# Layer four of a streaming encoder step: pooled projection, gate projection and group matmul alternated tile by tile

## The chip, the cores and the metric
One Trainium2 chip, all 8 cores, one program. Each core computes its own half of one prompt (2048 positions and their halo) and one sample request; the cores do not exchange data. The time is that of the slowest core, in microseconds of device time.

## The reference, cut to what matters
The trunk has four layers, each `x = x + gate * out`, with a different mixer. The layer in question is the fourth, multi-scale pooling:

```
h = rms_norm(x, g_norm[3]) * (1 + scale) + shift                  # 1024 channels
pv, z = split(h @ w_in_d, 2)                                       # 2048 channels each
ext = concat(history of 15 rows, pv)
dlt = trailing mean of ext over 2 / 4 / 8 / 16 rows (by channel group of 512) - pv
y = (dlt @ w_pool_d[g], for each of the four groups) * scale_pool_d
out = (y * silu(z)) @ w_out_d                                      # back to 1024
```
The last 15 rows of `ext` are outputs as well. Layers one to three and the final RMSNorm are unchanged.

## The kernel before
Channels lie on partitions, positions along the free axis. A core has 2128 positions (`NX`), in five tiles `t` with bounds `TB` (432, 384, 384, 512 and 416 columns; layer four leaves out the first 32 or 48 columns, so that its first tile has 400 or 384). The 2048 branch channels are 16 chunks `c` of 128; a pooling group `g` has four chunks, its window is `2 << g`.

The engines' instruction streams are written by one Python program in one order. `Sched` keeps for each named buffer who wrote it and who read it and adds semaphore waits; each engine then runs its own stream in that order. A buffer's key stands for the whole buffer, and keys whose memory overlaps exclude each other. Matmul results go through six PSUM banks in rotation (`next_bank`); banks 6 and 7 hold sums of squares.

Weights of 128 x 1024 come by GpSimd's queue into a ring of 20 slots in the order of `plan`; `done` gives a slot back, and the ring frees only from its oldest slot on.

Layer four before, for each group: a stage of pooled projections (four chunks by five tiles, eight matmuls each, `proj` and `mm8`, L458), a stage of gate projections (the same with Silu on the way out, L1047), a stage of group matmuls (four matmuls each, over the four pooled chunks `DL`, with the gate product L1059 on VectorE). In the pooled stage a tile goes through

- L1010 VectorE: copy the last 15 columns of the tile before into the head of this tile's buffer `tf` (L1007, a memset, for the first tile)
- L1012 ScalarE: evict the bank into `tf` behind the head (twice in the last tile, which has a second history for the sample)
- L1015, L1019, L1020, L1021 VectorE: mask, second history, rows to be kept (first or last tile only)
- L1027 VectorE: `g + 1` adds that double the window each time
- L1032 VectorE: scale and subtract into `DL[i]`; L1037 and L1039 correct the first 16 positions

The copy and the eviction write the same key `tf`, so the eviction waits for the copy. There are two `tf` buffers, and one set of four `DL` buffers that lies over the x buffers `XT` of the output projection. `out_proj` (L569 matmuls, L577 residual add, L507 square, L508 sum of squares) loads x tiles `xbuf` into these by SyncE's queue; after its last matmul of layer three it normalises the last tile into `HT` (L515, L516, L524, L526), which layer four's last tile reads.

Of the kernel before, what the change touches and what calls it, by code (L numbers as in the profile page):

```python
# [7 lines left out]
ALU = mybir.AluOpType  # L8
# [6 lines left out]
NX = 2128  # L15
HALO = 48
SMP = 2096
# [189 lines left out]
def build_program():  # L207
# [175 lines left out]
    for g in range(4):  # L383
        for j in (0, 1):
            for i in range(4):
                add(("in", 3, 16 * j + 4 * g + i), w_in_d[3][16 * j + 4 * g + i])
        for hf in range(2):
            add(("pool", g, hf), w_pool_d[2 * g + hf])
# [597 lines left out]
    def layer_d():  # L986
        TF = [tmp("tf%d" % i, i * 528, 528) for i in range(2)]
        SA = tmp("sa", 1056, 528)
        SB = tmp("sb", 1584, 528)
        T3 = tmp("t3", 2112, 16)  # L990
        DL = [xsb("dl%d" % i, 8192 - 1064 * (i + 1), NX, True) for i in range(4)]
        n = 0
        for g in range(4):
            win = 2 << g
            for i in range(4):
                c = 4 * g + i
                od = outD[c % 2]
                for t in range(NT):
                    x0, x1 = max(TB[t], 32), TB[t + 1]
                    w = x1 - x0  # L1000
                    tf, tf_old = TF[n % 2], TF[(n + 1) % 2]
                    n += 1
                    tail = (t == NT - 1)
                    b = proj(3, c, t, 32)
                    parts = [(0, w, 15)] if not tail else [(0, SMP - x0, 15), (SMP - x0, w, 30)]
                    if t == 0:
                        s.op("dve", lambda h, tf=tf: h.memset(tf.v[:, 0:15], 0.0), writes=[tf.key])  # L1007
                    else:
                        pw = x0 - max(TB[t - 1], 32)
                        s.op("dve", lambda h, tf=tf, tf_old=tf_old, pw=pw: h.tensor_copy(out=tf.v[:, 0:15], in_=tf_old.v[:, pw:pw + 15]), reads=[tf_old.key], writes=[tf.key])  # L1010
                    for (a, e, sh) in parts:
                        s.op("act", lambda h, b=b, tf=tf, a=a, e=e, sh=sh: h.activation(out=tf.v[:, a + sh:e + sh], in_=bank(b)[:, a:e], func=AF.Copy), reads=[], writes=bk(b) + [tf.key])  # L1012
                    wx = w + 15
                    if t == 0:
                        s.op("dve", lambda h, tf=tf: h.tensor_scalar_mul(out=tf.v[:, 15:31], in0=tf.v[:, 15:31], scalar1=maskc[:, 0:1]), reads=["par", tf.key], writes=[tf.key])  # L1015
                    if tail:
                        wx = w + 30
                        pe_ = SMP - x0 + 15
                        s.op("dve", lambda h, tf=tf, c=c, pe_=pe_: h.tensor_copy(out=tf.v[:, pe_:pe_ + 15], in_=stD[:, c, :]), reads=["par"], writes=[tf.key])  # L1019
                        s.op("dve", lambda h, tf=tf, pe_=pe_, od=od: h.tensor_copy(out=od[:, 0:15], in_=tf.v[:, pe_ - 15:pe_]), reads=[tf.key], writes=["outD%d" % (c % 2)])  # L1020
                        s.op("dve", lambda h, tf=tf, wx=wx, od=od: h.tensor_copy(out=od[:, 15:30], in_=tf.v[:, wx - 15:wx]), reads=[tf.key], writes=["outD%d" % (c % 2)])  # L1021
                        s.dma("sp", "o_d%d" % (c % 2), opd[c], od, reads=["outD%d" % (c % 2)], writes=["O.pd.%d" % c])
                    src, lo, sh = tf, 0, 1
                    for k in range(g + 1):
                        dst = SA if k % 2 == 0 else SB
                        lo2 = lo + sh
                        s.op("dve", lambda h, src=src, dst=dst, lo2=lo2, sh=sh, wx=wx: h.tensor_tensor(out=dst.v[:, lo2:wx], in0=src.v[:, lo2:wx], in1=src.v[:, lo2 - sh:wx - sh], op=ALU.add),  # L1027
                             reads=[src.key], writes=[dst.key])
                        src, lo, sh = dst, lo2, sh * 2
                    outs = [(max(a, 48 - x0), e, p) for (a, e, p) in parts]  # L1030
                    for (a, e, p) in outs:
                        s.op("dve", lambda h, src=src, tf=tf, a=a, e=e, p=p, i=i, x0=x0, win=win: h.scalar_tensor_tensor(  # L1032
                            out=DL[i].v[:, x0 + a:x0 + e], in0=src.v[:, a + p:e + p], scalar=1.0 / win, in1=tf.v[:, a + p:e + p], op0=ALU.mult, op1=ALU.subtract),
                            reads=[src.key, tf.key], writes=[DL[i].key])
                    if t == 0:
                        o = 15 + 16
# [3 lines left out]
                             reads=[T3.key, tf.key], writes=[DL[i].key])  # L1040
                done(("in", 3, c))
            for i in range(4):
                c = 4 * g + i
                for t in range(NT):
                    x0, x1 = max(TB[t], HALO), TB[t + 1]
                    b = proj(3, 16 + c, t, HALO)
# [130 lines left out]
```

How the kernel before makes its waits and increments, by code:

```python
        def emit(h):  # L128
            for sm, v in wl:
                h.wait_ge(sm, v)
            ins = fn(h)
            ins.then_inc(mysem, 1)
# [18 lines left out]
        def emit(h):  # L151
            for sm, v in wl:
                h.wait_ge(sm, v)
            h.dma_start(out=out, in_=in_).then_inc(dsm, 16)
# [9 lines left out]
        def emit(h):  # L164
            for sm, v in wl:
                h.wait_ge(sm, v)
```

## Time and profile before

| | us |
|---|---|
| median of 3 runs (lowest to highest) | 2855.18 (2853.37 to 3117.13) |
| the profiled execution | 2853.27 |
| its span on the slowest core (core 2) | 2851.7 |
| spans of the eight cores | 2838.4 to 2851.7 |
| mean granted TensorE clock, cores | 0.913 to 0.920 |
| layer four in the span | 2236.8 to 2674.5 |
| last output projection | from 2674.5 |

A clock of 1.00 is TensorE at 2.4 GHz, 0.50 at 1.2 GHz. In the rows, PE is TensorE's matmuls, PEld its weight loads, DVE VectorE, ACT ScalarE, POOL GpSimd, SP SyncE; `big` is SBUF, `ps` PSUM.

### The profile page before, as it was taken

What the parts mean: (1) busy time and instruction counts of PE and PEld (TensorE: products, weight loads), DVE (VectorE), ACT (ScalarE), POOL (GpSimd) and SP (SyncE); (2) the same over time, 40 slices, a digit from 0 to 9 for tenths busy, and PEclk for the clock granted to TensorE, in tenths of its full rate; (3) what the DMA queues carried; (4) which work ended last, traced back from release to release, by engine and by line L of the source; (5) the groups of instructions that cost most, each with busy time, mean ns of one, the idle gap of its engine ahead of it and who ended that gap; (6) DMA issues with size and microseconds to landing.
All of it is one profiled execution on the core that took longest, in us unless ns stands there. A gap on an engine that the chain in (4) does not pass through costs nothing.

```text
span 2851.7 us, 38831 instructions; the slowest of 8 cores (2838.4 to 2851.7 us)
## 1 busy us (share of the span) xinstructions
PE 2253.8 (79%) x12651; PEld 1200.2 (42%) x12651; DVE 1498.8 (53%) x2600; ACT 778.4 (27%) x1381; POOL 198.4 (7%) x373
## 2 busy tenths in 40 slices
PE   1396899977899999878688888867578687685976
PEld 0142555543455555443345454533243343341543
DVE  1466562233666666533566666567633444757343
ACT  2621233333311111132322222256522322121211
POOL 1001201100010101000000000000000100000000
PEclk9998899988999999988799998988788899897998
DMA  9300727534343433424543334234433421111132
GB/s 185 98 1 4 119 34 130 85 100 103 55 63 50 60 52 52 78 80 125 103 78 78 78 78 78 60 83 116 112 110 115 83 31 27 23 27 15 49 110 86
DMA packets 142851, 215.10 MB, mean 75 GB/s; under 512 B 14560, under 2 KB 83168, under 8 KB 141920
## 3 DMA queue, kind: packets, MB, share of 16 engines
q0 software_dynamic: 50544, 96.00, 22.8%
q1 hardware_dynamic: 92112, 116.63, 13.4%
q8 instruction: 106, 1.74, 0.2%
q14 instruction: 89, 0.73, 0.1%
HBM read 255.18 MB, written 53.40 MB: 108 GB/s over the span
## 4 chain that ended last, share of the span: by engine, by line
PE 58%; DVE 19%; ACT 10%; issue 6%; DMA 5%; POOL 1%; DVEq 1%; ACTq 0%; SPq 0%; POOLq 0%
PE ps L458 37%; PE ps L569 15%; DVE big L1027 4%; ACT big L526 3%; DVE big L516 2%; ACT big L953 2%; DVE big L681 2%; DVE big L1032 2%; ACT big L1012 2%; PE ps L508 2%; PE ps L879 1%; DVE big L915 1%; DMA big<-w_ada 1%; DVE big L524 1%; DMA big<-xbuf 1%
## 5 line engine op out<-in xcount | busy, mean ns | idle before, releaser
L458 PE MATMUL ps<-big 128*128 128x384 bf16 (+4 forms) x7360 | 1417.7, 352 | 206.7 <-ACT big L1012 104.4
L458 PEld LDWEIGHTS ps<-big 128*128 128x128 bf16 x7360 | 723.9, 100 | 841.0 <-issue 305.2
L569 PE MATMUL ps<-big 128*128 128x384 bf16 (+4 forms) x2560 | 522.7, 363 | 20.7 <-DVE big L966 20.7
L569 PEld LDWEIGHTS ps<-big 128*128 128x128 bf16 x2560 | 263.6, 103 | 255.8 <-issue 70.7
L577 DVE SCALAR_TENSOR_TENSOR big<-ps,big 128x384 f32<-128x384 f32 (+3 forms) x192 | 110.2, 582 | 406.6 <-PE ps L569 376.4
L507 ACT ACTIVATE big<-big 128x384 bf16<-128x384 f32 (+4 forms) x200 | 107.9, 554 | 510.1 <-DVE big L577 463.0
L508 PE MATMUL ps<-big 128*128 128x384 bf16 (+4 forms) x200 | 75.3, 397 | 211.3 <-ACT big L507 211.3
L915 DVE TENSOR_TENSOR big<-big,ps 128x384 bf16<-128x384 f32 (+1 forms) x96 | 160.1, 1668 | 106.0 <-ACT big L911 103.0
L526 ACT ACTIVATE big<-big 128x384 bf16<-128x384 f32 (+3 forms) x192 | 131.3, 684 | 94.8 <-DVE big L524 78.6
L1027 DVE TENSOR_TENSOR big<-big 128x398 f32<-128x398 f32 (+11 forms) x200 | 121.9, 610 | 57.6 <-ACT big L1012 42.4
L674 PE MATMUL ps<-big 128*128 128x512 bf16 (+1 forms) x576 | 129.2, 387 | 10.0 <-ACT big L677 5.4
L508 PEld LDWEIGHTS ps<-big 128*128 128x128 bf16 x200 | 20.2, 102 | 246.2 <-issue 235.4
L516 DVE RECIPROCAL big<-big 128x384 f32<-128x384 f32 (+4 forms) x25 | 70.3, 2812 | 101.5 <-ACT big L515 101.5
L818 ACT ACTIVATE big<-ps 128x384 bf16<-128x384 f32 (+3 forms) x80 | 42.0, 526 | 289.2 <-PE ps L458 289.1
L1012 ACT ACTIVATE big<-ps 128x384 f32<-128x384 f32 (+1 forms) x96 | 44.3, 462 | 270.4 <-DVE big L1010 177.5
L822 DVE SCALAR_TENSOR_TENSOR big<-big 128x384 f32<-128x384 f32 (+3 forms) x160 | 106.2, 664 | 17.0 <-DVE big L820 0.5
L879 PE MATMUL ps<-big 128*128 128x270 bf16 x640 | 108.9, 322 | 0.0
L807 DVE TENSOR_TENSOR big<-big,ps 128x384 f32<-128x384 f32 (+1 forms) x96 | 50.3, 524 | 99.0 <-PE ps L458 89.0
L886 ACT ACTIVATE big<-ps,big 128x270 bf16<-128x270 f32 x128 | 62.3, 486 | 140.4 <-DVE big L889 70.0
L911 ACT ACTIVATE big<-ps 128x384 f32<-128x384 f32 (+3 forms) x80 | 42.1, 527 | 210.5 <-PE ps L458 169.4
L893 PE MATMUL ps<-big 128*128 128x270 bf16 x128 | 40.3, 316 | 74.0 <-ACT big L886 73.5
L855 DVE TENSOR_TENSOR big<-big 128x1280 bf16<-128x1280 bf16 x64 | 94.7, 1486 | 2.0 <-PE ps L894 0.5
(105 smaller groups left out, 1678.9 us busy)
## 6 DMA issues: line engine op xcount, KB each, us to landing
big<-w_ada POOLq DMA_DIRECT2D x96, 256.0 KB, 6.6
big<-w_in_b POOLq DMA_DIRECT2D x64, 256.0 KB, 6.6
big<-w_in_c POOLq DMA_DIRECT2D x48, 256.0 KB, 5.4
big<-xbuf SPq DMA_DIRECT2D x7, 1536.0 KB, 8.9
xbuf<-big SPq DMA_DIRECT2D x48, 192.0 KB, 2.0
gbuf<-big SPq DMA_DIRECT2D x16, 548.0 KB, 6.3
big<-gbuf SPq DMA_DIRECT2D x16, 548.0 KB, 4.9
ybuf<-big SPq DMA_DIRECT2D x16, 540.0 KB, 2.7
```

Source lines behind the costliest of these rows:

```text
L458: ins = h.matmul(out, lhsT=lhs(k), rhs=rhs(k), start=(k == 0), stop=(k == n - 1))
L507: s.op("act", lambda h: h.activation(out=SQ[k].v[:, 0:w], in_=XT[q][d].v[:, 0:w], func=AF.Square), reads=[XT[q][d].key], writes=[SQ[k].key])
L508: return lambda: s.op("pe", lambda h: h.matmul(bank(b)[:, 0:w], lhsT=onesb, rhs=SQ[k].v[:, 0:w], start=(d == 0), stop=(d == 7)), reads=["o ...
L516: s.op("dve", lambda h: h.reciprocal(out=R.v[:, 0:w], in_=R.v[:, 0:w]), reads=[R.key], writes=[R.key])
L526: s.op("act", lambda h, X=X, d=d, a=a, b=b, sq=sq: h.activation(out=HT[:, d, 80 + a:80 + b], in_=X.v[:, a - x0:b - x0], func=AF.Identity, ...
L569: ins = h.matmul(bank(b)[:, 0:w], lhsT=w8[e // 8][:, e % 8, :], rhs=YS[:, e, x0:x0 + w], start=(e == 0), stop=(e == 15))
L577: s.op("dve", lambda h, b=b, X=X, a=a, e=e, sq=sq, d=d, x0=x0: h.scalar_tensor_tensor(out=X.v[:, a - x0:e - x0], in0=bank(b)[:, a - x0:e - ...
L674: ins = h.matmul(bank(p + j)[0:n, :], lhsT=HT[:, kc, c0:c0 + n], rhs=w[:, kc, :], start=(kc == 0), stop=(kc == 7))
L822: s.op("dve", lambda h, P=P, A=A, c=c, wx=wx, j=j: h.scalar_tensor_tensor(out=A.v[:, 0:wx], in0=P.v[:, j:j + wx], scalar=wcb[:, c, j:j + 1 ...
L879: ins = h.matmul(bank(b)[:, 0:YPH], lhsT=W.v[:, o:o + 128], rhs=GP.v[:, g * CPH + 4 - sh:g * CPH + 4 - sh + YPH], start=(sh == 0), stop=(s ...
L915: s.op("dve", lambda h, b=ba, sg=sg, a=a - x0, e=e - x0, m0=m0, M=M, G3=G3: h.tensor_tensor(out=G3[:, :, m0:m0 + M].rearrange("q p m -> q ...
L1027: s.op("dve", lambda h, src=src, dst=dst, lo2=lo2, sh=sh, wx=wx: h.tensor_tensor(out=dst.v[:, lo2:wx], in0=src.v[:, lo2:wx], in1=src.v[:, ...
```

## The change
Groups run in the order 8, 16, 4, 2 (`GORD = (2, 3, 1, 0)`). For each chunk and tile the program now issues a pooled projection with its VectorE work (`pv`), a gate projection (`zgate`), and, from the second group on, a group matmul with gate product of the group before (`pooled`). After the last group its group matmuls follow alone, tile by tile. Two sets `DLS` of four pooled chunks take turns; the first chunk of each set lies in scratch, the others over the x buffers. There are three `tf` buffers instead of two. The eviction is issued ahead of the history copy, and the head of `tf` has a key of its own (`"h" + tf.key`), so that the eviction no longer waits for the copy. The weight plan follows the new order.

```diff
+    GORD = (2, 3, 1, 0)
+    for g in GORD:
+        for i in range(4):
+            for j in (0, 1):
                 add(("in", 3, 16 * j + 4 * g + i), w_in_d[3][16 * j + 4 * g + i])
...
-        TF = [tmp("tf%d" % i, i * 528, 528) for i in range(2)]
+        TF = [tmp("tf%d" % i, i * 528, 528) for i in range(3)]
...
-        DL = [xsb("dl%d" % i, 8192 - 1064 * (i + 1), NX, True) for i in range(4)]
+        DLS = [[tmp("dl0.0", 2656, NX, True)] + [xsb("dl0.%d" % (i + 1), 1064 * i, NX, True) for i in range(3)],
+               [tmp("dl1.0", 3720, NX, True)] + [xsb("dl1.%d" % (i + 1), 8192 - 1064 * (i + 1), NX, True) for i in range(3)]]
...
+            b = proj(3, c, t, 32)
+            parts = [(0, w, 15)] if not tail else [(0, SMP - x0, 15), (SMP - x0, w, 30)]
+            for (a, e, sh) in parts:
+                s.op("act", lambda h, b=b, tf=tf, a=a, e=e, sh=sh: h.activation(out=tf.v[:, a + sh:e + sh], in_=bank(b)[:, a:e], func=AF.Copy), reads=[], writes=bk(b) + [tf.key])
+            if t == 0:
+                s.op("dve", lambda h, tf=tf: h.memset(tf.v[:, 0:15], 0.0), writes=["h" + tf.key])
+            else:
+                pw = x0 - max(TB[t - 1], 32)
+                s.op("dve", lambda h, tf=tf, tf_old=tf_old, pw=pw: h.tensor_copy(out=tf.v[:, 0:15], in_=tf_old.v[:, pw:pw + 15]), reads=[tf_old.key, "h" + tf_old.key], writes=["h" + tf.key])
...
+        for gi, g in enumerate(GORD):
+            for i in range(4):
+                for t in range(NT):
+                    pv(g, i, t, DLS[gi % 2])
+                    zgate(4 * g + i, t)
+                    if gi:
+                        pooled(GORD[gi - 1], i, t, DLS[(gi - 1) % 2])
+                done(("in", 3, 4 * g + i))
+                done(("in", 3, 16 + 4 * g + i))
+            if gi:
+                for hf in range(2):
+                    done(("pool", GORD[gi - 1], hf))
+        g = GORD[-1]
+        for t in range(NT):
             for fi in range(4):
+                pooled(g, fi, t, DLS[1])
+        for hf in range(2):
+            done(("pool", g, hf))
```
Where the diff has no lines, the arithmetic of a tile (mask, adds, subtraction, gate product) is the same as before.

## Rows read from the trace of the kernel before

**Rows 1.** Windows, core 2: engines' busy us, granted clock, DMA share, GB/s

```profile
2300.00:2338.00 38.00, 37.66 (x215) 20.87 (x216) 14.66 (x28) 11.35 (x22) 2.65 (x5) 1.00 0.20 29
...
2550.00:2637.60 87.60, 48.02 (x188) 19.68 (x187) 62.58 (x138) 10.71 (x24) 2.65 (x5) 0.77 0.15 21
...
2238.00:2683.50 445.50, 325.00 (x1630) 161.38 (x1628) 251.87 (x562) 95.52 (x197) 19.51 (x37) 0.90 0.19 32
```

**Rows 2.** Waits, 2238 to 2684 us: us in total, times, longest

```profile
ACT big L1012 <- DVE big L1010: 177.5, 62, 4.3
...
PE ps L458 <- ACT big L1012: 104.4, 59, 3.7
...
DVE big L1027 <- ACT big L1012: 42.4, 48, 7.3
...
DVE big L1019 <- ACT big L1012: 14.6, 15, 1.0
DVE big L1015 <- ACT big L1012: 13.3, 16, 1.3
```

**Rows 3.** Timeline of one tile, window 16: start, duration, instruction

```profile
2577.09 0.17 DVE L1010 COPY big<-big 128x15 f32<-128x15 f32 x1
2577.35 0.49 ACT L1012 ACTIVATE big<-ps 128x384 f32<-128x384 f32 x1 [4.30 <-DVE big L1010]
2577.94 2.58 DVE L1027 TENSOR_TENSOR big<-big 128x398 f32<-128x398 f32 x4 [0.69 <-ACT big L1012]
...
2580.63 0.56 DVE L1032 SCALAR_TENSOR_TENSOR big<-big 128x384 bf16<-128x384 f32 x1
2581.11 0.17 DVE L1010 COPY big<-big 128x15 f32<-128x15 f32 x1
```

**Rows 4.** Windows from one 512-column eviction L1012 to the next, VectorE alone

```profile
2346.15:2362.33 16.18, 10.53 (x27) 0.79 0.14 21
...
2446.57:2466.26 19.69, 13.56 (x32) 0.83 0.10 15
2562.31:2585.38 23.07, 16.56 (x37) 0.88 0.09 12
...
2259.07:2271.56 12.49, 7.47 (x22) 1.00 0.31 43
```

**Rows 5.** Timeline, VectorE, group matmuls' stage of window 4

```profile
2423.00 3.27 DVE L1059 SCALAR_TENSOR_TENSOR big<-ps,big 128x512 bf16<-128x512 f32 x5 [0.24 <-PE ps L458]
```

**Rows 6.** Timeline, ScalarE, gate projections: one tile of two neighbouring chunks

```profile
2407.41 0.49 ACT L1047 ACTIVATE big<-ps 128x384 bf16<-128x384 f32 x1 [0.78 <-PE ps L458]
...
2414.44 0.49 ACT L1047 ACTIVATE big<-ps 128x384 bf16<-128x384 f32 x1 [0.78 <-PE ps L458]
```

**Rows 7.** Timeline, start of layer four

```profile
2255.34 9.84 PE L458 MATMUL ps<-big 128*128 128x416 bf16 x45 [12.49 <-ACT big L526]
2255.57 0.57 DVE L1027 TENSOR_TENSOR big<-big 128x398 f32<-128x398 f32 x1 [7.33 <-ACT big L1012]
```

**Rows 8.** Timeline, start of the last output projection

```profile
2674.46 5.36 PE L569 MATMUL ps<-big 128*128 128x384 bf16 x32
...
2681.69 1.14 DVE L577 SCALAR_TENSOR_TENSOR big<-ps,big 128x384 f32<-128x384 f32 x2 [6.31 <-DMA big<-xbuf]
...
2688.80 2.84 PE L569 MATMUL ps<-big 128*128 128x384 bf16 x16
```

**Rows 9.** Timeline, TensorE, pooled stages of windows 2 and 16

```profile
2280.61 1.46 PE L458 MATMUL ps<-big 128*128 128x384 bf16 x8 [1.27 <-ACT big L1012]
...
2596.64 2.72 PE L458 MATMUL ps<-big 128*128 128x384 bf16 x8 [2.69 <-ACT big L1012]
```

**Rows 10.** Line L818, the Silu of layer two: its table loads

```profile
L818 ACT ACT_TABLE_LOAD  x1: 1283/1283/1283, 737.0 to 737.0; - x1
```

**Rows 11.** Window over layer two, columns as in rows 1

```profile
740.00:1180.00 440.00, 440.00 (x2615) 241.59 (x2614) 293.24 (x640) 79.93 (x152) 44.81 (x84) 1.00 0.36 51
```

**Rows 12.** The page's DMA issues: KB each, us to landing

```profile
big<-w_in_b POOLq DMA_DIRECT2D x64, 256.0 KB, 6.6
```

More of the change, by code:

```diff
@@ L382, in build_program @@
     add_out(2)
-    for g in range(4):
-        for j in (0, 1):
-            for i in range(4):
+    GORD = (2, 3, 1, 0)
+    for g in GORD:
+        for i in range(4):
+            for j in (0, 1):
                 add(("in", 3, 16 * j + 4 * g + i), w_in_d[3][16 * j + 4 * g + i])
@@ L986, in layer_d @@
     def layer_d():
-        TF = [tmp("tf%d" % i, i * 528, 528) for i in range(2)]
-        SA = tmp("sa", 1056, 528)
-        SB = tmp("sb", 1584, 528)
-        T3 = tmp("t3", 2112, 16)
-        DL = [xsb("dl%d" % i, 8192 - 1064 * (i + 1), NX, True) for i in range(4)]
-        n = 0
-        for g in range(4):
-            win = 2 << g
[L995 to L1036, printed above, removed]
-                        s.op("dve", lambda h, src=src, g=g, o=o: h.tensor_tensor(out=T3.v, in0=src.v[:, o:o + 16], in1=invc[:, g * 16:(g + 1) * 16], op=ALU.mult),
-                             reads=[src.key, "par"], writes=[T3.key])
-                        s.op("dve", lambda h, tf=tf, i=i, o=o: h.tensor_tensor(out=DL[i].v[:, 48:64], in0=T3.v, in1=tf.v[:, o:o + 16], op=ALU.subtract),
[L1040 to L1046, printed above, removed]
-                    s.op("act", lambda h, b=b, c=c, x0=x0, x1=x1: h.activation(out=YS[:, c, x0:x1], in_=bank(b)[:, 0:x1 - x0], func=AF.Silu), reads=[], writes=bk(b) + ["ys.%d.%d" % (c, t)])
-                done(("in", 3, 16 + c))
@@ L1049, in layer_d, with zgate, pooled @@
+        def zgate(c, t):
+            x0, x1 = max(TB[t], HALO), TB[t + 1]
+            b = proj(3, 16 + c, t, HALO)
+            s.op("act", lambda h: h.activation(out=YS[:, c, x0:x1], in_=bank(b)[:, 0:x1 - x0], func=AF.Silu), reads=[], writes=bk(b) + ["ys.%d.%d" % (c, t)])
+        def pooled(g, fi, t, DL):
             wp = [use(("pool", g, hf)) for hf in range(2)]
             wpv = [v3(v, 2) for v, _ in wp]
-            for fi in range(4):
-                c = 4 * g + fi
-                for t in range(NT):
-                    x0, x1 = max(TB[t], HALO), TB[t + 1]
-                    w = x1 - x0
-                    b = next_bank()
-                    item(mm8(bank(b)[:, 0:w], lambda k, fi=fi, wpv=wpv: wpv[k // 2][:, k % 2, fi * 128:(fi + 1) * 128], lambda k, x0=x0, x1=x1: DL[k].v[:, x0:x1], 4),
-                         [k for _, ks in wp for k in ks] + [DL[k].key for k in range(4)], bk(b))
-                    s.op("dve", lambda h, b=b, c=c, x0=x0, x1=x1, w=w: h.scalar_tensor_tensor(out=YS[:, c, x0:x1], in0=bank(b)[:, 0:w], scalar=pv_("spool")[:, c:c + 1], in1=YS[:, c, x0:x1],
-                                                                                             op0=ALU.mult, op1=ALU.mult), reads=["par", "ys.%d.%d" % (c, t)], writes=bk(b) + ["ys.%d.%d" % (c, t)])
@@ L1061, in layer_d @@
-            for hf in range(2):
-                done(("pool", g, hf))
+            c = 4 * g + fi
+            x0, x1 = max(TB[t], HALO), TB[t + 1]
+            w = x1 - x0
+            b = next_bank()
+            item(mm8(bank(b)[:, 0:w], lambda k: wpv[k // 2][:, k % 2, fi * 128:(fi + 1) * 128], lambda k: DL[k].v[:, x0:x1], 4),
+                 [k for _, ks in wp for k in ks] + [DL[k].key for k in range(4)], bk(b))
+            s.op("dve", lambda h: h.scalar_tensor_tensor(out=YS[:, c, x0:x1], in0=bank(b)[:, 0:w], scalar=pv_("spool")[:, c:c + 1], in1=YS[:, c, x0:x1],
+                                                         op0=ALU.mult, op1=ALU.mult), reads=["par", "ys.%d.%d" % (c, t)], writes=bk(b) + ["ys.%d.%d" % (c, t)])
```

40 lines of the change are left out of this document (added).

## The prediction

> **What bounds the kernel now.** I first found layer four in the trace. On core 2, the profiled one, it runs from 2236.8 to 2674.5 us of a span of 2851.7 us, and only it and the start of the last output projection are touched by the change. TensorE is busy 325 us of the 445.5 us around it, VectorE 252 us; neither is full [rows 1]. Split by stage, the gate projections and group matmuls run TensorE without a hole (37.66 busy of 38.00 us, clock 1.00), while the pooled projections of the last group leave it 48 us busy in 87.6, at a mean clock of 0.77 [rows 1]. So TensorE idles in one kind of stage and VectorE in the other, and neither idle time is used.
>
> The waits say what sets the pace of the pooled stages. ScalarE's eviction L1012 waited 177.5 us for the history copy L1010, and TensorE 104.4 us for that eviction; VectorE in turn waited for the eviction at L1027, L1019 and L1015 [rows 2]. The timeline of one tile shows the ring: history copy at 2577.09, eviction, four adds from 2577.94, the subtraction at 2580.63, the next copy at 2581.11 [rows 3]. A tile costs 4.02 us there, TensorE's eight matmuls take 1.46 of it at full clock [rows 9]. It is a chain of VectorE work with a round trip over ScalarE in it. A whole chunk (five tiles, from one 512-column eviction to the next) takes 12.49, 16.18, 19.69 and 23.07 us for windows 2, 4, 8 and 16, with VectorE busy 7.47, 10.53, 13.56 and 16.56 us [rows 4].
>
> **The change, part by part.** Number of matmuls, adds, evictions and bytes is the same; work is only reordered, so I price each new stage by the engine that fills it.
>
> *The round trip goes.* The eviction no longer stands behind the copy, and a third buffer lets it run two tiles ahead. VectorE waited for L1012 42.4 + 14.6 + 13.3 us; 7.3 of the first is the start of the layer. The other 63.0 us are 3.94 per chunk [rows 2]. Not all of it returns: the adds now follow the copy on VectorE itself, and between two dependent operations there lie 0.11 us (four adds end at 2577.94 + 2.58 = 2580.52, the next starts at 2580.63) [rows 3]. Five such gaps are 0.55, so a chunk gets 3.4 us shorter: 9.1, 12.8, 16.3 and 19.7 us of VectorE.
>
> *The gate products join in.* L1059 runs five in 3.27 us when it has a backlog [rows 5], 3.3 per chunk. Bounds: between VectorE's own operations they may overlap their neighbours (the subtraction of 0.56 us is followed by the copy after 0.48 [rows 3]), 2.9; or each takes a gap of 0.11 more, 3.8. I take 3.3, the row itself. VectorE per chunk with the gates: window 16 23.0, window 4 16.1, window 2 12.4; window 8, whose chunks come first, 16.3 without them.
>
> *TensorE per chunk.* Evictions of the same tile of two chunks of the gate projection lie 7.03 us apart (2407.41 to 2414.44) with TensorE full [rows 6]. The pooled projection has the same eight matmuls and 16 more columns, 7.1; the group matmul has four of eight, 3.5. Together 17.6, in the first group 14.1.
>
> *Which engine sets each stage.* First group (window 8): VectorE, 16.3 over 14.1. Second (16, with gates of 8): VectorE, 23.0 over 17.6. Third (4): TensorE, 17.6 over 16.1. Fourth (2): TensorE, 17.6 over 12.4. The rest, four chunks of group matmuls: TensorE, 14.1 over 13.2. This needs TensorE to run ahead. Six banks, three per tile, are two tiles of lead; what holds a bank longest is the gate product, which waits for nothing but its own matmul. Of each engine's queue: a late group matmul would hold up VectorE's next adds behind the gate product, but TensorE has it done a tile earlier; ScalarE has two evictions of about 0.5 us in a tile of 3.5 to 4.6 and is not near full.
>
> *Start.* ScalarE normalises the last tile's input after the layer has begun, and TensorE stood 12.49 us for it, until 2255.34 [rows 7]. The new first tile has three adds instead of one ahead of that work (1.35 us later), and a gate eviction and the next pooled eviction behind it, so VectorE resumes at about 2257.6 instead of 2255.6. The time TensorE could gain by gate projections meanwhile is worth nothing, since VectorE sets this group. From there: four chunks less the one tile done, 65.2 - 3.4 = 61.8, to 2319.4; second group 4 x 23.0 = 92.0, to 2411.4. TensorE enters the third group two projections ahead (2.7 us, all it can do before the group matmul needs the last chunk's final tile), but that matmul and the small difference of 17.6 and 16.1 make tiles catch on each other: I book 1.5 us back. 4 x 17.6 = 70.4, to 2480; fourth 70.4, to 2551; 2 us until the last tile's adds are through; 14.1, to 2567. Before: 2674.5. Gain 107.5 us.
>
> *End.* The first of the second chunk set no longer lies over the first x buffer, so x of tile 0 is loaded during the last group matmuls. Before, that load ended the wait at 2681.69, 6.31 us, and TensorE reached its fourth output item at 2688.80, 14.3 us after the first; that item's 16 matmuls took 2.84 [rows 8], so three with their two sum matmuls are 8.8. Gain 5.5. The load of tile 1 still waits for the last group matmul; it is wanted 22 us later, which hides its 7 us. If tile 0's load were not early, the 5.5 us are lost. SyncE's queue holds only the small outputs of kept rows ahead of it.
>
> *Clock.* In the stage of window 2, holes of 1.27 us between tiles [rows 9] went with a granted clock of 1.00 [rows 4]; after a hole of 2.69 us the eight matmuls took 2.72 instead of 1.46 us, half the clock [rows 9]. The new holes are (23.0 - 17.6) / 5 = 1.1 us on average in the second group, smaller elsewhere, but not even, since t3 and t4 differ. A tile at half clock costs TensorE 3.5 us, where it has 1.1 spare. Nothing to 10 us; I take 3, near the rows with small holes. In the third and fourth group there are no holes.
>
> *Free by cover.* The weights: the ring of 20 holds two pool slots, eight, two and eight, so while one group runs, the next one's is loaded; a slot's transfer took 6.6 us [rows 12] on a stage of 65. Evictions alternate Copy and Silu; layer two does the same and shows one table load of 1.283 us in its 455 us [rows 10], and there was one here before too, so nothing is added.
>
> Sum: 107.5 + 5.5 - 3 = 110 us. The profiled execution took 2853.3 us (1.6 beyond the span), the median is 2855.2. 2853.3 - 110 = 2743.3; with half of the 1.9 us between the two, 2744 us.
>
> **A rule of the Trainium skill against this.** In layer two TensorE was full for 440 us on this core, all cores running the same program, at a granted clock of 1.00 [rows 11]; and the 7.03 us per chunk of layer four [rows 6] are its 16640 columns at 2.4 GHz (6.93 us) and little more. The Trainium skill, page TensorE: Matmul & The Clock Gate, Part 1, "What's actually happening", says that once three cores of a die run dense matmuls the die goes to 13/16 of the clock. By that rule layer two would have shown 0.81; the trace disagrees, so the rule has a small chance here, as rival (a).
>
> **Rivals.**
>
> (a) TensorE's rate stays low when the holes close, as all neighbours become dense too. From the layer's own mean, 0.90, to its worst stage, 0.77 [rows 1], chunks of 17.6 become 19.6 to 22.9 us. Third and fourth group and the rest grow by 155 x (1/0.90 - 1) = 17 to 155 x (1/0.77 - 1) = 46 us, the first group by none to 4 x 2.0 = 8: 17 to 54, the middle 36: 2780 us. Against it stands layer two [rows 11]. 0.05. The rule of the Trainium skill, page TensorE: Matmul & The Clock Gate, is of this kind; an estimate from its 13/16 is 40 us, 2784.
>
> (b) The engines catch on each other: banks or the three buffers give less lead than counted, each tile loses 0.4 us (for scale: one step from VectorE's copy to ScalarE's eviction is 2577.09 to 2577.35, 0.26 us [rows 3], and a tile would pay it once or twice). 80 x 0.4 = 32 us: 2776 us. For it: tiles are uneven (384 to 512 columns, more small copies on the last). 0.12.
>
> (c) Weights late: as the group's two pool slots stay held through the next group, ten transfers go out at once at each boundary. If each of four boundaries waited for one landing, 4 x 6.6 [rows 12] = 26 us: 2770 us. 0.03.
>
> (d) The clock falls for good in the VectorE-bound groups: TensorE's chunk is 28.2 and 35.2 us, 4 x (28.2 - 16.3) + 4 x (35.2 - 23.0) = 96 us more: 2840 us, no change that can be told. Against it: at half clock TensorE would be full, and the full stretch from 2300 is at 1.00 [rows 1]. 0.04.
>
> (e) Slower: lock step. VectorE's gate product of a tile waits for its group matmul, that waits in TensorE's order behind two projections, and if the next pooled projection can only start when the gate product frees the bank, each tile is the sum: 3.5 TensorE + 0.5 ScalarE + 2.9 VectorE (mean of the four chunks, over 5) + 0.7 gate = 7.6 us. 80 tiles are 608 us instead of 438: some 3025 us. It decides as soon as the lead falls below one tile, and passes the old time from 5.4 us per tile on. Six banks speak against it. 0.03.
>
> That the change does not do what it says would be (e) or (b) in part.
>
> **Chances and range.** Forecast 0.73, (a) 0.05, (b) 0.12, (c) 0.03, (d) 0.04, (e) 0.03. The forecast's own bounds: gates -2 to +4, clock +3 to -7, hand-over between groups 4, the start 2, all of them rough, 2728 to 2762. To hold (b), (a) and (c) in most of their forms, and a DVE chain cheaper than I price it, the range is 2722 to 2786. Two per cent is what a measurement can tell from no change, 2798 us here: forecast, (a), (b), (c) lie below it, 0.92 with some spill; (d) and spill 0.05; (e) 0.03.
>
> **What would show it.** Right: VectorE over 95% occupied (busy plus its small gaps) in the first two groups, with a 512-column eviction to the next in about 16.3 and 23 us; TensorE full at 1.00 in groups three and four, 17.6 us per chunk; no wait of L1012 for the history copy; no wait of L577 for x. Wrong: VectorE waiting for L1012 or the group matmul in every tile (b, e), a clock below 0.9 in the first two groups (d), chunks of over 20 us with TensorE full (a), TensorE waiting for a weight transfer (c). The number is most exposed in VectorE's 154 us of groups one and two: 5% there are 8 us.

## The result, and the profile after

The changed kernel takes 2733.9 us (median of 4 runs, 2733.5 to 2736.8), against 2855.2 shown before; the ratio is 0.958, with a 95% interval of 0.9557 to 0.9603. The forecast was 2744, its range 2722 to 2786. Of the four runs of the kernel before in that comparison two were at 3112 and 3117 us with a lower clock on one die; they are left out of the ratio.

The page of the slowest core (7), its first lines: span, then each engine's busy time.

```profile
span 2731.4 us, 38776 instructions; the slowest of 8 cores (2721.2 to 2731.4 us)
PE 2212.5 (81%) x12651; PEld 1195.0 (44%) x12651; DVE 1493.1 (55%) x2600; ACT 781.4 (29%) x1381; POOL 197.7 (7%) x373
```

The engines' numbers of instructions are those of before; the span is 120.3 us shorter. Not all of that is waiting: on core 2 the same 1604 matmuls of layer four kept TensorE busy for 320.4 us before and for 291.0 after, because fewer of them ran at half clock. To compare the same core I use core 2 (span 2730.5, before 2851.7). Windows at the borders of the new stages: the start; groups 8, 16, 4 and 2; the last tile's adds; the remaining group matmuls; the output projection. Columns as in [rows 1].

```profile
2233.50:2255.80 22.30, 10.54 (x62) 5.79 (x60) 10.58 (x20) 12.30 (x22) 1.05 (x2) 0.85 0.47 95
2255.80:2316.30 60.50, 51.50 (x280) 27.75 (x281) 50.92 (x121) 19.81 (x44) 4.22 (x8) 0.92 0.25 36
2316.30:2404.80 88.50, 74.50 (x400) 39.05 (x400) 76.27 (x166) 21.45 (x44) 5.29 (x10) 0.96 0.07 10
2404.80:2474.50 69.70, 69.67 (x381) 38.04 (x382) 50.72 (x122) 19.93 (x41) 0.00 (x0) 0.96 0.16 28
2474.50:2543.70 69.20, 69.20 (x394) 38.37 (x392) 42.66 (x108) 20.75 (x42) 5.30 (x10) 1.00 0.24 40
2543.70:2547.30 3.60, 2.10 (x12) 1.00 (x11) 2.04 (x7) 1.21 (x3) 0.96 (x2) 1.00 0.03 4
2547.30:2561.50 14.20, 14.19 (x81) 7.93 (x82) 12.31 (x20) 0.00 (x0) 3.28 (x7) 1.00 0.99 194
2561.50:2730.50 169.00, 128.05 (x681) 68.63 (x678) 64.52 (x95) 25.89 (x46) 0.00 (x0) 0.89 0.30 98
```

The reader is to see who is full where. In the groups of windows 4 and 2 TensorE is busy all the time (69.67 of 69.70, 69.20 of 69.20). In those of 8 and 16 it is not; there VectorE shows 50.92 of 60.50 and 76.27 of 88.50, which looks like 85% but is all it can do: after 2256.25, where it resumes, it waits for no other engine in either group, and the rest lies in gaps of about 0.1 us between its own dependent operations. The timeline of one tile of window 16 shows it (start, duration), the successor of [rows 3]:

```profile
2323.82 0.56 DVE L1033 SCALAR_TENSOR_TENSOR big<-big 128x384 bf16<-128x384 f32 x1
2324.09 0.49 ACT L1008 ACTIVATE big<-ps 128x384 f32<-128x384 f32 x1 [1.51 <-PE ps L459]
2324.30 0.61 DVE L1057 SCALAR_TENSOR_TENSOR big<-ps,big 128x384 bf16<-128x384 f32 x1
2324.83 0.17 DVE L1013 COPY big<-big 128x15 f32<-128x15 f32 x1
2325.10 2.58 DVE L1028 TENSOR_TENSOR big<-big 128x398 f32<-128x398 f32 x4
...
2327.78 0.56 DVE L1033 SCALAR_TENSOR_TENSOR big<-big 128x384 bf16<-128x384 f32 x1
```

From subtraction to subtraction 3.96 us, with a gate product in it, against 4.02 without one before. The adds start 0.27 us after the copy (0.85 before). The eviction now runs during the tile before, and in this tile it waits for TensorE, not for the copy. The waits of the layer, the successor of [rows 2]:

```profile
ACT big L1008 <- PE ps L459: 95.6, 51, 9.3
...
DVE big L1028 <- ACT big L1008: 32.4, 22, 9.2
...
ACT big L1008 <- DVE big L1013: 13.2, 8, 2.5
PE ps L459 <- DVE big L1016: 12.2, 3, 9.0
PE ps L459 <- ACT big L1046: 11.8, 1, 11.8
...
PE ps L459 <- DVE big L1033: 7.3, 2, 5.8
```

177.5 us of eviction waiting for the copy have become 13.2 (by the program, a copy that still reads the buffer which the eviction is to fill), and TensorE's waits for the eviction, 104.4, are gone. Of VectorE's 32.4 us for L1008, 23.2 lie in the groups in which TensorE is the bound, and cost nothing; the other 9.2 are one wait at the start of the layer, behind ScalarE's normalisation, and they are on the path. What TensorE still waits for: 11.8 us at the start, 9.0 and 5.8 us at the ends of the two groups that VectorE sets (for the last pooled chunk), 1.5 us before the last group matmuls, and holes of 0.4 to 1.6 us within the group of window 16. The granted clock of TensorE, in finer windows of TensorE alone:

```profile
2320.80:2400.00 79.20, 70.02 (x387) 1.00 0.01 2
2404.80:2409.60 4.80, 4.77 (x16) 0.50 1.12 185
2409.60:2474.50 64.90, 64.90 (x367) 1.00 0.09 17
```

So the small holes within the group of window 16 left the clock at 1.00. The mean of 0.96 in this group and in the next comes from two stretches at half clock, one of 4.5 us (2316.3 to 2320.8) after the hole of 9.0 us and one of 5 us after the hole of 5.8 us.

The end of the layer, the successor of [rows 8]:

```profile
2546.19 15.81 SPq L154 DMA_DIRECT2D big<-xbuf  x2
2546.34 4.24 POOL L154 DMA_DIRECT2D big<-w_out_d  x8 [63.21 <-PE ps L459]
...
2547.31 14.23 PE L459 MATMUL ps<-big 128*128 128x384 bf16 x80 [1.51 <-DVE big L1033]
...
2561.38 5.36 PE L570 MATMUL ps<-big 128*128 128x384 bf16 x32
2564.25 0.62 DVE L578 SCALAR_TENSOR_TENSOR big<-ps,big 128x384 f32<-128x384 f32 x1 [1.95 <-PE ps L570]
...
2569.50 2.76 PE L570 MATMUL ps<-big 128*128 128x384 bf16 x16
```

The x load of tile 0 goes out at 2546.19, before the last group matmuls; L578 waits for its own matmul alone, and the fourth output item begins 8.1 us after the first, not 14.3.

**A measure that depends less on the chip.** I take the layer's length from the start of the first pooled eviction to the start of the last gate product, and the rest from there to the end of the span. Both come from the lines' first and last starts; for core 4, after:

```profile
L1008 ACT ACTIVATE big<-ps x96: 197/490/646, 2234.5 to 2543.0; 128x384 f32<-128x384 f32 x48, 128x400 f32<-128x400 f32 x16, 128x512 f32<-128x512 f32 x16, 128x32 f32<-128x32 f32 x16
L1057 DVE SCALAR_TENSOR_TENSOR big<-ps,big x80: 607/618/752, 2319.1 to 2560.2; 128x384 bf16<-128x384 f32 x48, 128x512 bf16<-128x512 f32 x16, 128x416 bf16<-128x416 f32 x16
```

2560.2 - 2234.5 = 325.7. Over the eight cores it is 325.6 to 325.9 after and 435.9 to 436.2 before; the rest is 168.5 to 168.9 after, and before it is 176.9 to 177.1 on seven cores and 180.6 on core 4, where the wait for x was 11.0 us instead of 6.3. So of the 120.3 us between the slowest cores' spans (core 2 before, core 7 after), 110.2 are the layer, 8.4 the output projection, and 1.7 an earlier part that the change doesn't touch.

### The profile page after: what moved, and what is told of

It is laid out like the page before. It is cut to its first block, busy times and chain, and to the rows that moved or that the text cites. A ratio compares the mean times of both kernels' runs of the same rounds, so it can differ in the third digit from the quotient of the medians.

```text
span 2731.4 us, 38776 instructions; the slowest of 8 cores (2721.2 to 2731.4 us)
## 1 busy us (share of the span) xinstructions
PE 2212.5 (81%) x12651; PEld 1195.0 (44%) x12651; DVE 1493.1 (55%) x2600; ACT 781.4 (29%) x1381; POOL 197.7 (7%) x373
## 4 chain that ended last, share of the span: by engine, by line
PE 62%; DVE 17%; ACT 9%; issue 6%; DMA 5%; POOL 1%; DVEq 1%; ACTq 0%; SPq 0%; POOLq 0%
PE ps L459 40%; PE ps L570 16%; ACT big L527 3%; DVE big L1028 3%; DVE big L517 2%; ACT big L954 2%; DVE big L682 2%; PE ps L509 2%; PE ps L880 2%; DVE big L916 1%; DMA big<-w_ada 1%; DVE big L525 1%; DVE big L951 1%; DVE big L950 1%; DMA big<-xbuf 1%
## 5 line engine op out<-in xcount | busy, mean ns | idle before, releaser
L459 PE MATMUL ps<-big 128*128 128x384 bf16 (+4 forms) x7360 | 1380.6, 347 | 125.8 <-ACT big L976 49.0
L570 PE MATMUL ps<-big 128*128 128x384 bf16 (+4 forms) x2560 | 517.4, 360 | 25.7 <-DVE big L967 25.7
L578 DVE SCALAR_TENSOR_TENSOR big<-ps,big 128x384 f32<-128x384 f32 (+3 forms) x192 | 110.2, 582 | 401.1 <-PE ps L570 371.0
L509 PE MATMUL ps<-big 128*128 128x384 bf16 (+4 forms) x200 | 74.9, 395 | 210.6 <-ACT big L508 210.6
L954 ACT ACTIVATE big<-big 128x270 bf16<-128x270 f32 x128 | 78.6, 614 | 55.0 <-DVE big L951 43.9
```

The lines of the kernel that those rows point to most:

```text
L459: ins = h.matmul(out, lhsT=lhs(k), rhs=rhs(k), start=(k == 0), stop=(k == n - 1))
L509: return lambda: s.op("pe", lambda h: h.matmul(bank(b)[:, 0:w], lhsT=onesb, rhs=SQ[k].v[:, 0:w], start=(d == 0), stop=(d == 7)), reads=["o ...
L570: ins = h.matmul(bank(b)[:, 0:w], lhsT=w8[e // 8][:, e % 8, :], rhs=YS[:, e, x0:x0 + w], start=(e == 0), stop=(e == 15))
L578: s.op("dve", lambda h, b=b, X=X, a=a, e=e, sq=sq, d=d, x0=x0: h.scalar_tensor_tensor(out=X.v[:, a - x0:e - x0], in0=bank(b)[:, a - x0:e - ...
L954: s.op("act", lambda h, g=g, i=i: h.activation(out=ZB.v[:, g * YPH:(g + 1) * YPH], in_=LTb.v[:, g * YPH:(g + 1) * YPH], func=AF.Silu, scal ...
```

## The experiments

Lengths of layer four in us, lowest and highest of the eight cores of each profiled run; ratios are to the kernel before on the same chip, with 95% intervals. "Staged" is the order of the kernel before: all pooled projections of a group, then all its gate projections, then all its group matmuls; `tf` are the buffers that the eviction fills.

| kernel | layer four | ratio |
|---|---|---|
| before | 435.9 to 436.2 | |
| changed | 325.6 to 325.9 | 0.958 (0.9557 to 0.9603) |
| e1 staged, eviction ahead, three tf | 361.0 to 361.2 | 0.9744 (0.9728 to 0.9759) |
| e7 staged, eviction ahead, two tf | 369.4 to 369.6 | 0.9754 (0.969 to 0.9819) |
| e2 changed, copy first | 358.6 to 360.2 | 0.9704 (0.9683 to 0.9725) |
| e3 changed, group matmuls staged | 342.8 to 343.2 | 0.9651 (0.9634 to 0.9668) |
| e4 changed, order 2, 4, 8, 16 | 321.5 to 321.8 | 0.9568 (0.9551 to 0.9585) |
| e5 changed, x late | 325.6 to 325.9 | 0.962 (0.9551 to 0.969) |
| e6 changed, two tf | 325.6 to 325.8 | 0.9584 (0.9551 to 0.9616) |
| e9 changed, again | 325.6 to 325.8 | 0.9575 (0.9526 to 0.9624) |
| e8, e10 three gate projections ahead | 303.2 to 306.2 | 0.9497 (0.9455 to 0.954), 0.9536 (0.9497 to 0.9575) |
| e11 and the start filled | 312.4 to 317.1 | 0.9569 (0.9523 to 0.9615) |

On the chips of e5 to e11 the layers before this one took up to 46 us longer on some cores, in the kernel before too (its fastest runs were 2885 and 2862 us); this widens the intervals. The length of layer four in the changed kernel is the same there to 0.3 us (e5, e6, e9), so I judge those runs by it.

**e1, the eviction ahead alone**, in the staged kernel.

```diff
-        TF = [tmp("tf%d" % i, i * 528, 528) for i in range(2)]
+        TF = [tmp("tf%d" % i, i * 528, 528) for i in range(3)]
...
                     parts = ...
+                    (eviction of the bank into tf, writes tf.key)
                     if t == 0: (memset of the head)   else: (history copy)
-                    ... writes=[tf.key]
+                    ... writes=["h" + tf.key]
-                    (eviction of the bank into tf, writes tf.key)
```

> The staged kernel before, with only the eviction ahead of the history copy, a key of its own for the head and three tf buffers. If the round trip over ScalarE costs what I priced (3.4 us a chunk, read from the changed kernel 3.9), 16 chunks give 54 to 62 us: 2791 to 2799 us, and VectorE's chunks take 12.2, 15.8 and 18.9 us for windows 4, 8 and 16, window 2 8.6. Rival, that the alternation brings the gain and the round trip is filled anyway: under 15 us, 2840 us or more.

Measured 0.9744, which is 73 us off 2853, and a layer 75.0 us shorter. On core 0 the chunks take 8.5 to 9.1, 12.3 to 12.6, 15.7 to 15.9 and 19.1 to 20.0 us for windows 2, 4, 8 and 16, the last somewhat longer than expected. The round trip was there to be had, and the rival is out; but the gain is 13 us more than 62. e7 looks for the rest.

**e7, the same with two tf buffers** (against e1).

```diff
-        TF = [tmp("tf%d" % i, i * 528, 528) for i in range(3)]
+        TF = [tmp("tf%d" % i, i * 528, 528) for i in range(2)]
...
-                    tf, tf_old = TF[n % 3], TF[(n + 2) % 3]
+                    tf, tf_old = TF[n % 2], TF[(n + 1) % 2]
```

> The staged kernel with the eviction ahead and two tf buffers (the first experiment had three and gained some 11 us more than the round trip of 3.9 us a chunk). If that rest is the lead of one tile that the third buffer gives TensorE into each gate stage, it falls away here: 2789 to 2793 us. If it is from somewhere else: 2780 us.

The time (0.9754, interval 0.969 to 0.9819) tells nothing; the layer is 369.5, 66.6 us shorter than before and 8.4 longer than e1. So 8.4 of the 13 us are the third buffer's. On core 0, 5.8 of them lie in the three passages over the gate stages (from the last 512-column eviction of a group to the first of the next: 135.4 us in e1, 141.3 in e7), while chunks inside the stage of window 8 take 15.8 us in both: mostly the lead into the gate stages, as supposed. 4.6 more than 62 remain. They too lie in these passages, 157.8 us before (core 2) and 141.3 in e7, of which three round trips are only 11.7; what makes them is not shown.

**e2, the changed kernel with the copy first again.**

```diff
+            if t == 0: (memset, writes tf.key)   else: (history copy, writes tf.key)
             for (a, e, sh) in parts: (eviction, writes tf.key)
-            if t == 0: (memset, writes "h" + tf.key)   else: (history copy, writes "h" + tf.key)
```

> The changed kernel, with the history copy ahead of the eviction again and one key for both. My theory: the round trip returns in the groups that VectorE sets, 4 x 3.9 in each of the first two, and makes VectorE the bound of the third (19.1 against 17.6, 6 us); the fourth stays TensorE's: 38 us more, about 2772 us. Rival, that the alternation alone covers the round trip: at most 5 us more, 2739 us.

Measured 0.9704, 2768 us; the layer is 33 to 34.5 us longer than changed, somewhat less than the 38 expected. 512-column evictions, one per chunk, of the groups of 8, 16 and 4 on core 0:

```profile
2259.20 0.60 ACT L1013 ACTIVATE big<-ps 128x512 f32<-128x512 f32 x1 [2.55 <-DVE big L1011]
2278.82 0.60 ACT L1013 ACTIVATE big<-ps 128x512 f32<-128x512 f32 x1 [2.55 <-DVE big L1011]
...
2367.61 0.60 ACT L1013 ACTIVATE big<-ps 128x512 f32<-128x512 f32 x1 [3.67 <-DVE big L1011]
2393.51 0.60 ACT L1013 ACTIVATE big<-ps 128x512 f32<-128x512 f32 x1 [3.67 <-DVE big L1011]
...
2460.25 0.60 ACT L1013 ACTIVATE big<-ps 128x512 f32<-128x512 f32 x1 [2.34 <-DVE big L1011]
2479.09 0.60 ACT L1013 ACTIVATE big<-ps 128x512 f32<-128x512 f32 x1 [2.34 <-DVE big L1011]
```

19.62, 25.90 and 18.84 us a chunk, against 15.8, 22.2 and 17.6 of the changed kernel: a chunk of the first two groups pays 3.7 to 3.8 us, and one of the third 1.2, as VectorE has become the bound there. Alternation does not cover a round trip that lies inside VectorE's own chain.

**e3, group matmuls in stages of their own.**

```diff
             for i in range(4):
                 for t in range(NT):
                     pv(g, i, t, DLS[gi % 2])
                     zgate(4 * g + i, t)
-                    if gi:
-                        pooled(GORD[gi - 1], i, t, DLS[(gi - 1) % 2])
+            for t in range(NT):
+                for fi in range(4):
+                    pooled(g, fi, t, DLS[gi % 2])
```

> The changed kernel, with pooled and gate projections alternating, but each group's matmuls in a stage of their own after it. My theory: the stages add up as 63 + 76 + 56 + 56 for the alternating part, four stages of 14.2 and four waits of some 3 us for the last pooled chunk: 15 to 20 us more than changed, 2749 to 2754 us. Rival, that the alternation of the group matmuls is where the gain lies: over 40 us more, 2775 us.

0.9651, 2753 us by the ratio; the layer is 17.4 us longer than changed: the sum holds, its parts don't all. TensorE's waits ahead of the first two group stages are not 3 us each:

```profile
2308.84 61.51 PE L459 MATMUL ps<-big 128*128 128x384 bf16 x332 [11.62 <-DVE big L1033]
...
2405.77 72.30 PE L459 MATMUL ps<-big 128*128 128x384 bf16 x395 [20.46 <-DVE big L1033]
2481.02 72.23 PE L459 MATMUL ps<-big 128*128 128x384 bf16 x395 [2.94 <-DVE big L1033]
```

In the groups that VectorE sets, TensorE had run ahead and stood 11.62 and 20.46 us before the group matmuls. I read that as the surplus of VectorE's work collected at one place; part of it comes back while the next group starts.

**e4, the order of the groups.**

```diff
-    GORD = (2, 3, 1, 0)
+    GORD = (0, 1, 2, 3)
```

> The changed kernel with the groups in the order 2, 4, 8, 16. Sum of the stages by the engine that is the bound: first group TensorE 56, where it works through the normalisation's wait, then 70, 76 and 89 (VectorE in the last two), the last tile's adds 5, 14: some 6 us less to 3 us more than changed, 2728 to 2737 us. Rival, that the order 8, 16, 4, 2 matters as the light groups then cover the heavy one: 13 us or more slower, 2747 us.

The layer is 4 us shorter (the times' intervals overlap; the median was 2729.4 us): the changed order is not the better one. With window 2 first, TensorE works without a hole for 182 us from its restart on, so VectorE's pause during the normalisation costs less; what this order pays is the end, where the last pooled tile of window 16 holds up TensorE for 8.43 us (core 4) and the 80 matmuls behind that hole take 17.06 us instead of 14.23.

**e5, x of tile 0 late.** The sets change places, so the last group's chunks lie over the first x buffer.

```diff
-                    pv(g, i, t, DLS[gi % 2])
+                    pv(g, i, t, DLS[(gi + 1) % 2])
...
-                pooled(g, fi, t, DLS[1])
+                pooled(g, fi, t, DLS[0])
```

> The changed kernel with the two chunk sets swapped, so that the last group's chunks lie over the first x buffer and x of tile 0 can only be loaded after the last group matmul, as before. My theory: the stall at the first residual add returns, 5.5 us as booked, 8 if all that the last output projection got shorter by is this: 2739 to 2742 us. Rival, that the output projection got shorter for another reason (its clock): no change, 2734 us.

The time tells nothing (0.962, interval 0.9551 to 0.969). The layer's length is unchanged, and the rest after it is 174.7 to 178.0 us instead of 168.5 to 168.9. On core 0:

```profile
2558.98 5.36 PE L570 MATMUL ps<-big 128*128 128x384 bf16 x32
2559.23 1.00 SPq L154 DMA_DIRECT2D big<-xbuf  x2
2566.44 1.14 DVE L578 SCALAR_TENSOR_TENSOR big<-ps,big 128x384 f32<-128x384 f32 x2 [6.54 <-DMA big<-xbuf]
```

The wait is back, 6.5 us here and 8.6 on core 1, and the rest grows by 6 to 9 us. But the 8.4 us by which the output projection got shorter are not all this load. On core 2 TensorE reached tile 1 of the output projection 28.2 us after its start before and 21.9 after: 6.3 us. The other 2.1 come later, with no such wait: behind the later holes the 16 matmuls of an item took 6.31 us before and 4.78 after in one place (mean granted clock 0.56 and 0.75), 5.08 and 4.31 in another (0.57 and 0.68). Whether the change did that or chance did is not shown; with x late it did not come back.

**e6, two tf buffers in the changed kernel.**

```diff
-        TF = [tmp("tf%d" % i, i * 528, 528) for i in range(3)]
+        TF = [tmp("tf%d" % i, i * 528, 528) for i in range(2)]
...
-            tf, tf_old = TF[cnt[0] % 3], TF[(cnt[0] + 2) % 3]
+            tf, tf_old = TF[cnt[0] % 2], TF[(cnt[0] + 1) % 2]
```

> The changed kernel with two tf buffers instead of three. My theory: two are enough once the eviction is ahead, as ScalarE evicts a tile (0.5 us) while VectorE works on the one before (over 3 us): under 4 us more, 2734 to 2738 us. Rival, that the third buffer gives the lead that lets TensorE run ahead in VectorE's groups: 10 us or more, 2744 us.

The same layer to 0.1 us. The third buffer, worth 8.4 us in the staged kernel, is worth nothing here.

**e8 and e10, gate projections moved to where TensorE has time.** `ZX` names chunks whose gate projection is issued early: chunk 0 over the tiles of the first group, 1 and 2 over those of the second; the weight plan follows.

```diff
+    ZX = {0: [0], 1: [1, 2]}
...
                     pv(g, i, t, DLS[gi % 2])
-                    zgate(4 * g + i, t)
+                    if 4 * g + i not in ZC:
+                        zgate(4 * g + i, t)
+                    k += 1
+                    while m < k * nx // 20:
+                        zgate(*xq[m])
...
+                        m += 1
```

> The changed kernel, with three gate projections of the last group (window 2) done ahead, one chunk spread over the tiles of the first group and two over those of the second, in which TensorE has to wait for VectorE. My theory of who sets each stage: the first two groups keep their length (TensorE 63 of 62, 84 of 88.5), the last falls from 70 to 50: 19 us less, 2715 us. Rival, that what holds TensorE there is not spare time but the queues' coupling, so that added matmuls lengthen the group: no gain or worse, 2734 us or more.

> The kernel with three gate projections ahead, beside the changed one on one chip: layer four some 303 us, the time 21 us less than changed, 2713 us; ratio to before about 0.950. Rival, that its gain was the chip's: no difference to changed.

Twice the layer is 303.2 to 306.2 us, 19.5 to 22.6 shorter than changed, with ratios of 0.9497 and 0.9536. Beside e9 on one chip (0.9575) the times' intervals overlap; the layer's length doesn't. e10 on core 2, TensorE's stretches of work with the hole ahead of each:

```profile
2291.87 58.54 PE L465 MATMUL ps<-big 128*128 128x512 bf16 x320 [11.80 <-ACT big L1052]
2352.32 48.97 PE L465 MATMUL ps<-big 128*128 128x384 bf16 x280 [1.91 <-DVE big L1022]
2401.46 17.15 PE L465 MATMUL ps<-big 128*128 128x384 bf16 x96 [0.17 <-DVE big L1019]
2419.14 18.98 PE L465 MATMUL ps<-big 128*128 128x384 bf16 x104 [0.53 <-DVE big L1022]
2440.83 69.41 PE L465 MATMUL ps<-big 128*128 128x384 bf16 x392 [2.72 <-DVE big L1039]
2511.13 48.25 PE L465 MATMUL ps<-big 128*128 128x384 bf16 x272 [0.89 <-ACT big L1014]
2560.89 14.23 PE L465 MATMUL ps<-big 128*128 128x384 bf16 x80 [1.51 <-DVE big L1039]
```

Nothing is left on this core but 11.8 us at the start and 7.7 us in six holes. TensorE is the bound of the layer from end to end; by the layer's length and by the ratio this is the fastest kernel of the study.

The length has two values here, though: 303.3 to 303.4 us on four cores of e10 and 306.1 to 306.2 on the other four. The holes are the same; the clock is not. Core 0, the stretch behind the same hole of 2.72 us as in the fifth row above:

```profile
2403.65 71.01 PE L465 MATMUL ps<-big 128*128 128x384 bf16 x388 [2.72 <-DVE big L1039]
```

There the granted clock is 0.51 for the first 3.4 us, and it fell after the hole of 2.20 us at the start of window 16 too; on core 2 it stays at 1.00 behind its holes of 1.91 and 2.72. Each fall costs 1.4 to 1.7 us.

**e9, the changed kernel again**, for comparison on the chip of e10 and e11.

> The changed kernel as it is, to have it on the chip of the next two: layer four (first pooled eviction to last gate product) 325.7 us as before, and about 2734 us if the chip's other layers take as long.

325.6 to 325.8 us for the layer; the time was 32 us above 2734, all ahead of the layer.

**e11, the start filled.** Two things change at once. The eight pieces of the last tile's normalisation are deferred to one per item of layer four, and gate projections of chunks 0 and 9 for the first four tiles stand ahead of the first last-tile item.

```diff
+                        if l == 2 and t == NT - 1:
+                            make_h_spread(l + 1, t, x0, w, sg)
...
+    ZX = {0: [0, 9], 1: [1, 2]}
...
+                    if gi == 0 and i == 0 and t == NT - 1:
+                        for c in ZX[0]:
+                            for tt in range(NT - 1):
+                                zgate(c, tt)
```

> As the one before, but the normalisation of the last tile is spread over the first items of layer four, with the evictions of the first tiles between its pieces, and two chunks' gate projections (of windows 2 and 8) stand ahead of the first last-tile item. My theory: TensorE's 11.8 us at the start come from full banks behind ScalarE's block; it falls to 2 to 4 us, VectorE starts some 10 us earlier, and layer four falls from 303 to 293 to 296 us. Rival, that the pieces, now behind VectorE's adds, come later and TensorE waits as long for the last tile's input: 303 us or more.

312.4 to 317.1 us, slower than e10 by 6 to 14: my expectation fell. Core 4:

```profile
2272.03 2.94 PE L469 MATMUL ps<-big 128*128 128x384 bf16 x16 [3.21 <-ACT big L1069]
2278.51 6.04 PE L469 MATMUL ps<-big 128*128 128x512 bf16 x16 [3.54 <-ACT big L1069]
2286.00 48.45 PE L469 MATMUL ps<-big 128*128 128x384 bf16 x272 [1.46 <-ACT big L1069]
2346.32 67.34 PE L469 MATMUL ps<-big 128*128 128x384 bf16 x376 [11.87 <-DVE big L1039]
```

The start's hole did shrink (8.2 us in three), but 11.87 us appeared at the end of the group. VectorE sets this group, and its pieces and adds now took turns with ScalarE at each step: its adds of the second, third and fourth tile waited 1.77, 2.80 and 3.19 us for evictions, and the last tile 8.13 us, together 15.9 us where e10 has one wait of 9.2. The rival had the sign right and the place only in part: what came late was VectorE's work. Which of the two changes does it, the spread pieces or the gate projections ahead of the last tile, was not separated, nor were the pieces tried in another order.

## Which parts of the prediction held and which step failed, point by point

The mechanism held; the sum fell short, 110 us forecast against 120.3 between the spans. The step that failed is the price of VectorE's chunk in the first two groups. The prediction booked 153.8 us for them (61.8 and 92.0), with 3.4 us a chunk for the round trip and 3.3 for the gate products; the trace shows 148.6 (2256.25 to 2404.8), with 3.9 and 3.0. That is half of what was missing. The other terms follow.

- *Which engine sets each stage*: right in all five stages, from work per chunk alone. TensorE's chunk was 17.64 us in both groups that it sets, 17.6 booked.
- *The round trip goes*, the largest mis-sized term: a chunk got 3.9 us shorter, not 3.4 (15.8 in window 8 instead of 16.3). I had taken one dependence gap off for each of five tiles; but the mask of the first tile and the second history of the last write behind the head and do not depend on the copy under the new key, so these two tiles kept nothing of the wait. In window 8 the time from the operation ahead of the wait to the one behind it fell by 0.8 us in the first tile and 1.1 in the last, where VectorE had waited 0.7 and 1.0, and by 0.6 to 0.8 in the other three, where it had waited 0.7 to 0.9. In e2 the term, put back, costs 3.8. Eight chunks: 4 us.
- *The gate products join in*: 3.0 us a chunk instead of 3.3. In the tile shown each takes 0.53 us of VectorE's time (2324.30 to 2324.83) and not its own 0.61, so the lower bound, 2.9, was the better one. Group of 16: 88.5 us instead of 92.0, both terms together.
- *Start*: VectorE resumed at 2256.25 with the layer 2.7 us earlier in the span, so relative to it 1.4 us later than forecast. The prediction had put the table load for Silu at nothing, since there was one before. There was, at 2299.9, and TensorE waited 0.3 us in all for the gate evictions behind it; now it stands at 2253.9, between the normalisation and the first gate eviction, with the pooled evictions that VectorE waits for behind it, and takes 1.28 us.
- *TensorE's two groups and the hand-over*: from its restart at 2404.83 to the last group matmuls at 2547.31 it took 142.5 us, 141.6 booked. The 1.5 us for tiles catching on each other did not show, and the hole before the last group matmuls is 1.5 us, not 2. Against that stands the half clock of the next point.
- *Clock*: 3 us were booked, for small holes in the group of 16. Those left the clock at 1.00. What was paid is about 2.5 us at another place: the 5 us at half clock behind the hole of 5.8 us, at the start of a group that TensorE sets. The stretch at half clock behind the hole of 9.0 us cost nothing that shows, as VectorE sets that group. That the size was near is luck.
- *End*: 8.4 us instead of 5.5. Of these 6.3 are the wait for x, near what was booked; the load took longer on other cores (a wait of 6.5 and 8.6 us in e5, 11.0 on core 4 before), and I had read one core. The other 2.1 are the clock behind later holes, which the prediction did not look at.
- *Free by cover*: the weights and SyncE's queue were free; no wait of TensorE for a transfer is in the trace.
- *Rivals*: (a) is out by the clock of 1.00 in TensorE's two groups, (d) by the 1.00 in VectorE's, where it fell only behind the hole at the start and the two at the groups' ends. (c) is out by the absence of waits for transfers, (b) and (e) by full engines. The trace shows eight cores in the same dense layer at 1.00 from 2415 to 2540. The rule of the Trainium skill (page TensorE: Matmul & The Clock Gate, Part 1, "Seeing it yourself") that dense matmuls on three cores of a die bring 13/16 of the clock is again not what this trace shows.

The sum again, in us beyond the forecast's 110: VectorE's two groups +5.2, start -1.4, TensorE's two groups and the hand-over -0.9 (with the 2.5 of half clock in it), the clock term that was booked apart +3, end +2.9, and 1.7 from an earlier part that the change doesn't touch. Together 120.5; the spans say 120.3.

What the parts of the change are worth depends on the order in which they are added. Added in one order, by the lengths: eviction ahead 66.6 (before to e7), third buffer 8.4 (e7 to e1, and nothing once tiles alternate), gate with pooled projections together with the order of the groups and two sets of chunks 18.0 (e1 to e3), group matmuls 17.4 (e3 to changed). In the other order, all the rest comes first: 76 to 77.5 (before to e2), and the eviction ahead then adds 33 to 34.5 (e2 to changed), as it counts only where VectorE sets the pace. The early x load is 6.3 behind the layer in either. So each half alone, the first with its third buffer, brought about two thirds of the layer's 110 us. That the sum came near says little about this: the prediction had not priced the parts apart.

## What to carry to other kernels

Price a reordering per stage, by the fuller engine's time including the gaps between its dependent operations, and look for round trips to another engine inside that engine's chain: here a key of its own for 15 columns, alone, brought about as much as the interleaving of three stages alone (66.6 and 8.4 more with a third buffer, against 76 to 77.5 us). Once each stage has one full engine, the next gain is to move free-standing work of that engine's kind from the stages where it is the bound to those where it is not (19.5 to 22.6 us here); filling a hole of an engine that doesn't set the stage only moved the hole in e11. Judge such changes by the length of the stage on all cores. It repeated to 0.3 us for the changed kernel while whole times differed by 30. In other kernels it spread by 1.6 us between cores in e2, 2.9 in e10 and 4.7 in e11, and in e10 the granted clock of TensorE was the cause.

## What the runs showed of the hardware

- VectorE's operations with no dependence between them start before the one ahead has ended: the gate product of 0.61 us was followed by the copy after 0.53, the subtraction of 0.56 by the gate product after 0.48.
- VectorE's dependent operations lie about 0.1 us apart (2577.94 + 2.58 to 2580.63 before). With these gaps VectorE, waiting for no other engine, shows 76.27 us busy of 88.50.
- Seven holes of TensorE of 0.4 to 1.6 us in 79 us went with a granted clock of 1.00 (2320.8 to 2400). After holes of 9.0 and 5.8 us the clock was 0.50 for 4.5 and 5 us; after a hole of 8.43 us in e4 the last 80 matmuls took 17.06 us instead of 14.23.
- Behind a hole of 2.72 us the same kernel (e10) had 0.51 for 3.4 us on core 0 and 1.00 on core 2. Such falls made 303.4 us into 306.1.
- ScalarE's table load for Silu took 1.28 us: before at 2299.9, where TensorE waited 0.3 us for the evictions behind it, after at 2253.9, on the path.
- The layers ahead of this one took 38 us longer on core 1 of e9 than on core 1 of the changed kernel's first profile, with 1837.5 us of TensorE busy for the same matmuls instead of 1795.3 and a granted clock of 0.91 instead of 0.93; this dense layer had the same length on both to 0.3 us. What the early layers lost their clock to was not tried.
